# Hybrid decoder step on one NeuronCore: 88 instead of 64 early value tiles, and the slots at which the dense sums are taken

## What is computed

```python
def block(hb):                                            # 128 tokens of D_MODEL = 2048
    q = (hb @ w_query).reshape(TOK_BLOCK, PEER_HEADS, 2, D_QHALF)
    sc = jnp.einsum('thpc,pnc->thpn', q, sub_keys)
    ...                                                   # 8 heads x 16 best of 128 x 128 experts
    u = expert_u[idx]
    act = jax.nn.gelu(jnp.einsum('thkd,td->thk', u, hb), approximate=False)
    coef = (gate * act).astype(hb.dtype)
    return jnp.einsum('thk,thkd->td', coef, expert_v[idx])
```

## Time and profile before

| | |
|---|---|
| median of 3 runs | 3790.84 us (3784.7 to 3790.84) |
| the profiled execution | 3779.13 us |
| its span, first to last instruction | 3777.4 us |
| TensorE busy | 3104.6 us (82%) |
| VectorE busy | 2353.0 us (62%) |
| ScalarE, GpSimd busy | 572.1 us (15%), 980.1 us (26%) |
| moved by DMA | 1344.80 MB, mean 356 GB/s |
| granted TensorE clock, mean | 0.903 of 2.4 GHz |

### The profile page before, as it was taken

One profiled execution on the slowest core, in us unless ns is written; L12 is line 12 of the kernel. 1 busy time (PEld: TensorE's weight loads), 2 busy tenths in 40 slices (PEclk: granted clock), 3 DMA queues, 4 the chain that ended last, 5 costly groups with the idle time before them and its releaser, 6 DMA issues.

```text
span 3777.4 us, 28728 instructions
## 1 busy us (share of the span) xinstructions
PE 3104.6 (82%) x9975; PEld 1850.8 (49%) x9975; DVE 2353.0 (62%) x3580; ACT 572.1 (15%) x1365; POOL 980.1 (26%) x779
## 2 busy tenths in 40 slices
PE   4899997979996668796885885359996589999996
PEld 1333443733343434333674553347773257777774
DVE  3110114889986854548777777877777838656653
ACT  0000111121111445402242000420000000000000
POOL 3000001234333421233313323333223314222220
PEclk8999998979998679897996997579998899999998
DMA  9999655889989799988989999889999989999993
GB/s 310 398 361 367 233 200 202 338 319 403 409 330 361 262 401 415 397 296 336 367 292 358 416 416 386 283 341 417 417 417 416 416 333 417 416 417 417 417 411 132
DMA packets 326129, 1344.80 MB, mean 356 GB/s; under 512 B 27625, under 2 KB 76777, under 8 KB 217593
## 3 DMA queue, kind: packets, MB, share of 16 engines
q0 software_dynamic: 106912, 749.72, 49.8%
q1 hardware_dynamic: 166090, 549.84, 37.9%
q10 hardware_dynamic: 52984, 43.42, 3.5%
HBM read 1303.07 MB, written 38.96 MB: 355 GB/s over the span
## 4 chain that ended last, share of the span: by engine, by line
PE 57%; DMA 20%; DVE 15%; issue 4%; ACT 3%; POOL 0%; SPq 0%; ACTq 0%; DVEq 0%; POOLq 0%
PE ps L1023 27%; PE ps L619 7%; DVE arena L2183 7%; DMA arena<-in_expert_u_dram,arena 6%; DMA arena<-in_expert_v_dram 5%; PE ps L778 4%; PE ps L828 4%; DMA arena<-in_cache_k_dram 3%; PE ps L710 3%; PE ps L577 2%; DMA arena<-in_w_ada_dram 2%; DMA arena<-in_w_in_dram 2%; PE ps L607 2%; PE ps L1015 2%; DMA arena<-in_w_out_dram 1%
## 5 line engine op out<-in xcount | busy, mean ns | idle before, releaser
L1023 PE MATMUL ps<-arena 128*128 128x512 f32 x3072 | 1384.4, 611 | 175.2 <-DMA arena<-in_expert_v_dram 116.1
L2183 DVE CUSTOM_DVE_ANT_0 arena<-arena 128x2048 f32<-128x2048 f32 x544 | 1241.7, 2290 | 315.3 <-DMA arena<-in_expert_u_dram,arena 309.5
L1023 PEld LDWEIGHTS ps<-arena 128*128 128x128 f32 x3072 | 943.6, 309 | 615.0 <-issue 270.9
L2448 POOL DMA_INDIRECT arena<-in_expert_u_dram,arena x544 | 760.6, 1398 | 1760.9 <-DVE arena L2183 1567.0
L2096 DVE SCALAR_TENSOR_TENSOR arena<-arena 128x2048 f32<-128x2048 f32 x158 | 371.6, 2352 | 205.3 <-issue 165.8
L828 PE MATMUL ps<-arena 128*128 128x512 f32 x896 | 409.4, 611 | 0.4 <-DVE arena L2027 0.2
L619 PE MATMUL ps<-arena 128*128 128x512 f32 x640 | 288.4, 604 | 9.5 <-DMA arena<-in_w_in_dram 9.5
L828 PEld LDWEIGHTS ps<-arena 128*128 128x128 f32 x896 | 169.7, 195 | 246.6 <-issue 240.1
L2448 POOL DMA_INDIRECT arena<-in_expert_v_dram,arena x160 | 176.7, 1105 | 410.5 <-DVE arena L2096 368.3
L577 PE MATMUL ps<-arena 128*128 128x128 f32 (+3 forms) x954 | 158.4, 319 | 151.7 <-DMA arena<-in_cache_k_dram 50.3
L577 PEld LDWEIGHTS ps<-arena 128*128 128x128 f32 (+3 forms) x954 | 128.0, 169 | 220.2 <-issue 67.7
(11 more groups left out here) (246 smaller groups left out, 1761.1 us busy)
## 6 DMA issues: line engine op xcount, KB each, us to landing
arena<-in_expert_v_dram SPq DMA_DIRECT2D x320, 512.0 KB
arena<-in_w_ada_dram SPq DMA_DIRECT2D x96, 1024.0 KB, 10.5
arena<-in_w_in_dram SPq DMA_DIRECT2D x80, 1024.0 KB, 8.2
arena<-in_w_query_dram SPq DMA_DIRECT2D x36, 1024.0 KB
arena<-dense_coefs SPq DMA_DIRECT2D x48, 768.0 KB
arena<-in_w_out_dram SPq DMA_DIRECT2D x32, 1024.0 KB, 5.1
dense_coefs<-arena ACTq DMA_DIRECT2D x12, 2048.0 KB, 20.4
arena<-in_cache_k_dram SPq DMA_DIRECT2D x24, 1024.0 KB
```

What stands on the lines that cost most here:

```text
L1023: ins = MM(ps[:, BANK[half, b] + c, :], weights, dense_v[m % V_DENSE][:, c * NC:(c + 1) * NC], start=(m == FIRST_TILE[half, b]), stop=(m = ...
L2183: V.tensor_tensor_reduce(out=u_slot[s % RING], in0=u_slot[s % RING], in1=h2[b], scale=1.0, scalar=0.0, op0=ALU.mult, op1=ALU.add, accum_ou ...
L2448: nc.gpsimd.indirect_dma_start(out=slot, out_offset=None, in_=table, in_offset=bass.IndirectOffsetOnAxis(ap=idx, axis=0),).then_inc(loaded ...
```

## The change

It sets the number of early tiles from 64 to 88, gives them due times 1.2 slots apart instead of spreading them up to block 2's first quad (88 tiles then end at slot 395.2, quads at 399.3), and takes the low sums at slot 477 instead of 474, the high sums at slot 562 instead of 569.

```diff
-EARLY_TILES = 64
+EARLY_TILES = 88
...
 def t_tile(m):
     if m < EARLY_TILES:
-        return t_quad(1, QUADS) + 3.0 + (C_FROM[2] - t_quad(1, QUADS) - 4.0) * m / EARLY_TILES
+        return t_quad(1, QUADS) + 3.0 + 1.2 * m
     return t_quad(2, QUADS) + 2.0
...
-T_LOW = 474
-T_HIGH = 569
+T_LOW = 477
+T_HIGH = 562
```

## The result

The changed kernel took 3823.26 us (median of 5, 3810.42 to 3826.16), the kernel before 3784.7 us on the same chip (median of 5, 3780.0 to 3790.84). The ratio is 1.0088, with a 95% interval of 1.0067 to 1.0109: slower by 25 to 41 us. The forecast was +33 us, 3824.

A forecast was written before the change was run, and what follows sets the result against it. It took DMA to be full in most stages and to price the single tiles, with the end set by the low half plus 660 us of high tiles. Terms 10 + 8 + 5 + 0 + 10 = +33 us gave 3824; range 3780 to 3855.

The forecast's parts named there:

- More early tiles before the turns: Stretch before block 2's turns: 16 more early tiles share DMA with the gathers and slow the slots; +10 us (3 to 14).
- Eight tiles among the products: Block 2's quads: tiles in TensorE's order make products late and VectorE wait; +8 us (-11 to +27).
- Low half: Full and single tiles plus VectorE's stop: cheaper tiles about offset by three slots of later stop; 574 against 569 us, +5.
- High half: High tiles: same tiles, TensorE full at full clock, fewer gathers to disturb it; 0 us.
- The end: After the last tile: VectorE stops in slot 562 with five adds undone; 44.4 against 34.3 us, +10 (0 to +14).
- Rival A: Single tiles of the late low half run at TensorE's pace, so the kernel is faster, 3763 us; chance 0.12.
- Rival B: Both insertions of early tiles are hidden by a rising clock and spare DMA; no change, +3 us, 3794; chance 0.12.
- Rival C: Tiles among block 2's products run at half clock, 6.8 us each; +46 us more, 3870; chance 0.08.

The follow-up runs named there:

- e1: The change (88 early tiles) without its two due times, low and high sums at 474 and 569 as before; ratio 1.0032 to the kernel before.
- e8: The change's 88 early tiles with low sums at slot 466 and high sums at 563; ratio 0.9969 to the kernel before.
- e11: The kernel before, 64 early tiles, with its last eight moved among block 2's products, sums as before; ratio 1.0003.
- e5: 80 early tiles, all ahead of block 2's turns, none among its products, sums at 474 and 569 as before; ratio 1.0009 to the kernel before.
- e3: The kernel before with only the low sums moved, from slot 474 to 477; ratio 1.0043.
- e4: The kernel before with only the low sums moved, from slot 474 to 466; ratio 0.995.

## Why the prediction was right, step by step

The sum was +33, the ratio says +33 (25 to 41). That the two times agree to a microsecond (3824 and 3823.26) is luck: the forecast stood on a kernel before of 3790.84 us, which was 3784.7 beside the change, and the medians are 38.6 us apart. Less the 15 us by which its first tile came later, the profile has the first full tile at 2532 and the last tile at 3764, where 2532 and 3766 were forecast. The terms, against the means of the profiles with equal parts:

- *More early tiles before the turns*, forecast +10 (3 to 14). The change has 349.4 us against 337 to 341 with 64 tiles (six profiles): +11. The slower slots were right (3.85 us in the filled gap, 3.93 forecast), and by VectorE's step ahead of the turns they cost some 10 us in the mean of the six kernels with 80 or more tiles there. What the text took as settled, that TensorE is free and the turns find it ready, held by 1.9 us in the change and not in e1 and e8 (352.0 and 354.3): there 4 and 8 us come on top, which no term had.
- *Eight tiles among the products*, +8 (-11 to 27). 130 against 122 us, +8.6. The mechanism was the named one: TensorE's order, with VectorE waiting for products. It is shown in the profiles by e11, without more loads in all, and by e5, without the insertions; the time of e11 does not show it clear of noise. In the timeline of the change tile and product alternate, and the product behind a tile is late:

```profile
2433.31 3.72 PE L1023 MATMUL ps<-arena 128*128 128x512 f32 x8
2436.87 1.95 PE L1015 MATMUL ps<-arena 128*128 128x128 f32 x16
2440.55 1.16 PE L1015 MATMUL ps<-arena 128*128 128x128 f32 x8 [1.73 <-ACT arena L1424]
2441.54 3.72 PE L1023 MATMUL ps<-arena 128*128 128x512 f32 x8
```

- *Low half*, +5: 574 forecast, 572.6 measured; 4.47 us a single tile forecast, 4.45 measured; a stop of 48 us forecast, 45.6 measured. It is two effects of opposite sign, now apart: e1 has -10 for the tiles, and the three slots of `T_LOW` cost 12 (e3) to 14 us (e1 to the change), 4 to 5 us a slot. One reading was off without harm: that a full tile costs 5.19 us because it shares DMA. It costs 5.16 us in the high half too, with TensorE busy throughout; only the single tile is priced by DMA.
- *High half*, 0: -1.
- *The end*, +10: 42.3 and 42.7 us against 32 to 34, +9 to +10. High sums and adds took 19.8 us (19.9 forecast), scalings 7.3 (7.6), the sample's sums 8.3 (8.4), and what follows them 6.8 (8.5).

Rival A (the low half at TensorE's pace) fell: the single tiles kept 4.45 us, 133 GB/s for 590 KB. The Trainium skill has each DMA engine go round the queues that have work, a packet at a time (DMA: Bandwidth & Descriptors, section Queues, rings and completion order). With the packet sizes of the earlier trace rows that gave 133 GB/s, and here the trace agrees in the number. That working takes the packets which the profile counts, averaged over the whole program, for the packets of the rule; no run shows that they are the same. For early tiles it does not agree: 515 records in 273 us are 4.24 us a tile, 154 GB/s, as before; in the change 80 tiles were through in time.

Rival B (hidden insertions) was right in its premise only. The granted clock did rise in the quads, from 0.65 to 0.86, with TensorE busy 72 of 100 us instead of 55 of 89. The Trainium skill (TensorE: Matmul & The Clock Gate, Part 1) has the clock throttled by default and released by activity, and the trace agrees. With it the median record of a product fell from 421 to 275 ns (minimum, median and maximum at L1015, before and with the change):

```profile
L1015 PE MATMUL ps<-arena x256: 274/421/582, 2398.6 to 2483.8; 128*128 128x128 f32 x128
```

```profile
L1015 PE MATMUL ps<-arena x256: 272/275/583, 2422.6 to 2516.4; 128*128 128x128 f32 x128
```

The quads still grew, so faster products did not make up for the place of the tiles. Rival C (cold tiles) fell: five of the eight ran in 3.72 us, the others in 4.28 to 4.58, where 6.8 were feared.

The step on which the text was thinnest is the second: +8 was chosen between -11 and +27, and no row had quads with tiles among them. The profiled change is 44 us longer than the profiled kernel before; 15 of these lie ahead of the first tile, in scatter that the change does not touch and whose cause stays open, and the other 29 are within the interval.

## What to carry to other kernels

Before work is moved to relieve an engine, ask at what rate it runs where it will stand: these tiles needed a third of the matmuls and took 86% of the time, since TensorE set the pace of the one kind and DMA that of the other. Where two streams share a full DMA and it has room later, the moment at which one of them stops to wait is a lever on the other: here three slots later cost 12 to 14 us, and stopping six to eight sooner, together with the end fitted to it, gained 20 to 25. A due time set ahead of a wait moves behind it whatever follows on that engine; look at what is undone there.

## What the runs showed of the hardware that was not expected

Two loads of unequal row size, gathers of 8 KB rows and SyncE's 4 KB rows, split a full DMA at about 2 to 1 in bytes: 132 to 133 GB/s of 416 for SyncE in single tiles and 139 in full tiles, in both kernels, as the rows had it. Beside gathers of one table alone SyncE had 153 to 154 in both (150 in e8); why it gets more there is not shown. Not expected by the prediction was what the high half bears: with DMA at 406 instead of 384 GB/s over it (e4), TensorE's 128 tiles took 659.7 us instead of 660.7.

With tiles among them the same products took 275 instead of 421 ns in the median (a granted clock of 0.86 instead of 0.65 over the quads), but that was not enough to pay for 3.7 us tiles put in front of them.
